# Output projections' last tiles on banks of their own, and the Vector work around them in a different order

## The reference, cut to what matters

```python
for i in range(DEPTH):
    h = _rmsnorm(x, attn_norm[i])
    x = x + mixer_i(h, ...)            # attention, then o @ w_o (1024 x 1024)
    x = x + swiglu_ffn(_rmsnorm(x, ffn_norm[i]), w_gate[i], w_up[i], w_down[i])
return _rmsnorm(x, final_norm)
```

## Time and profile before

| | us |
|---|---|
| median of 3 runs | 1173.62 (1172.78 to 1173.78) |
| the profiled execution | 1172.65 |
| its span, first to last instruction | 1170.8 |
| mean granted TensorE clock over the span | 0.998 |

### The profile page before, as it was taken

The page is one execution under the profiler, slowest core; times in us unless marked ns, Lnnn a source line. Parts: engine busy times, 40 slices in busy tenths (PEclk is TensorE's granted clock), DMA queues, the critical chain, the costliest instruction groups (busy, mean ns, idle before and its releaser), DMA issues.

```text
span 1170.8 us, 18043 instructions
## 1 busy us (share of the span) xinstructions
PE 1155.0 (99%) x7336; PEld 1030.4 (88%) x7336; DVE 800.4 (68%) x864; ACT 632.5 (54%) x753; POOL 276.4 (24%) x251
## 2 busy tenths in 40 slices
PE   9999999999999999999999999999999999999997
PEld 7989988888997888888899888888889999888886
DVE  5786777775589667776558777766556867776642
ACT  6775565554455556555336746555346755655532
POOL 2200532211123354221111354221110005322100
PEclk9999999999999999999999999999999999999999
DMA  8743555555552346556553245555545335555650
GB/s 330 191 143 109 180 179 195 182 202 191 179 171 104 111 177 216 181 181 216 180 180 136 98 166 214 183 179 213 183 172 186 108 109 181 180 188 181 223 182 36
DMA packets 31260, 202.36 MB, mean 173 GB/s; under 512 B 3552, under 2 KB 4640, under 8 KB 7760
## 3 DMA queue, kind: packets, MB, share of 16 engines
q1 hardware_dynamic: 28800, 196.88, 47.7%
q10 hardware_dynamic: 2032, 3.07, 0.9%
q0 software_dynamic: 352, 1.31, 0.8%
HBM read 198.43 MB, written 1.84 MB: 171 GB/s over the span
## 4 chain that ended last, share of the span: by engine, by line
PE 93%; DVE 3%; ACT 2%; DMA 1%; SPq 1%; issue 1%; POOL 0%; ACTq 0%; DVEq 0%
PE banks L1321 38%; PE banks L1325 20%; PE banks L1309 9%; PE banks L1315 7%; PE banks L1317 6%; PE banks L1316 6%; PE banks L1447 1%; PE banks L1389 1%; DMA raw<-w 1%; PE banks L1461 1%; ACT w_hi L487 0%; PE banks L1449 0%; PE banks L1601 0%; DVE small L1147 0%; SPq L313 0%
## 5 line engine op out<-in xcount | busy, mean ns | idle before, releaser
L851 DVE TENSOR_TENSOR w_lo<-raw,w_hi 128x2048 fp32r<-128x2048 f32 x180 | 442.1, 2459 | 206.2 <-ACT w_hi L487 206.1
L487 ACT ACTIVATE w_hi<-raw 128x2048 fp32r<-128x2048 f32 x183 | 349.2, 1909 | 94.7 <-PE banks L1317 35.7
L1321 PE MATMUL banks<-x_split,w_hi 128*128 128x512 f32 x1408 | 336.7, 391 | 0.0
L1321 PEld LDWEIGHTS banks<-x_split,w_hi 128*128 128x128 f32 x1408 | 258.6, 188 | 49.8
L1325 PEld LDWEIGHTS banks<-x_split,w_lo 128*128 128x128 f32 x1408 | 181.1, 191 | 7.1
L1325 PE MATMUL banks<-x_split,w_lo 128*128 128x256 f32 x1408 | 184.0, 284 | 0.0
L1321 PE MATMUL banks<-hid_split,w_hi 128*128 128x512 f32 x528 | 129.9, 392 | 0.0
L1321 PEld LDWEIGHTS banks<-hid_split,w_hi 128*128 128x128 f32 x528 | 95.6, 188 | 17.4
L1315 PE MATMUL banks<-x_split,w_hi 128*128 128x256 f32 x384 | 110.8, 288 | 0.0
L1316 PE MATMUL banks<-x_split,w_hi 128*128 128x256 f32 x384 | 108.7, 283 | 0.0
L1317 PE MATMUL banks<-x_split,w_lo 128*128 128x256 f32 x384 | 108.7, 283 | 0.0
(11 more groups left out here) (194 smaller groups left out, 1573.7 us busy)
## 6 DMA issues: line engine op xcount, KB each, us to landing
raw<-w SPq DMA_DIRECT2D x183, 1024.0 KB, 4.9
raw<-w SPq DMA_DIRECT2D x8, 256.0 KB, 6.7
x<-x_in SPq DMA_DIRECT2D x4, 256.0 KB, 6.5
raw<-w SPq DMA_DIRECT2D x2, 512.0 KB, 7.9
k_all<-k_all ACTq DMA_DIRECT2D x1, 960.0 KB, 8.3
rel_scratch<-rel_lut POOLq DMA_DIRECT2D x1, 768.0 KB, 10.0
rel_bias<-rel_scratch POOLq DMA_DIRECT2D x2, 256.0 KB, 9.8
y_gain<-final_rows ACTq DMA_DIRECT2D x1, 512.0 KB, 3.5
```

Source lines behind the costliest of these rows:

```text
L487: act.activation(w_hi[slot][:, :], raw[slot][:, :], ACT.Copy).then_inc(hi_done, 1)
L851: dve.tensor_tensor(w_lo[slot][:, :], raw[slot][:, :], w_hi[slot][:, :].bitcast(FP32), ALU.subtract).then_inc(lo_done, 1)
L1321: return pe.matmul(pair(b), wt[0], xs, start=first, stop=False, skip_group_check=True)
```

## The change

The bank table and the signal that counts finished even tiles:

```diff
-GATE_BANKS, UP_BANKS, DOWN_BANKS, OUT_LAST_BANK = (0, 2), (4, 6), (2, 3), 3
+GATE_BANKS, UP_BANKS, DOWN_BANKS, LAST_BANKS = (0, 2), (4, 6), (2, 3), (2, 3, 6, 7)
-        norm = signals("norm", "six x_new hi lo ss sums ms guess rstd")
+        norm = signals("norm", "even x_new hi lo ss sums ms guess rstd")
```

VectorE's `out_projection`: tiles 4 to 7 have two adds, with a wait between them (`step`), and the low part of the first up unit is written ahead of add 6:

```diff
                 def add(t):
-                    if t == 6:
-                        dve.wait_ge(norm.six, i + 1)
+                    if t in (4, 6):
+                        dve.wait_ge(norm.even, 2 * i + t // 2 - 1)
                     else:
                         dve.wait_ge(unit_used, u + t // 2 + 1)
-                    src = bank[OUT_LAST_BANK][:, 0:SEQ] if t == 7 else pair(4 + t // 2 % 2)[:, t % 2, :]
+                    if t >= 4:
+                        step(dve.tensor_tensor(x[:, t, :], pair(LAST_BANKS[t - 4])[:, 1, :], x[:, t, :], ALU.add))
+                    src = pair(LAST_BANKS[t - 4])[:, 0, :] if t >= 4 else pair(4 + t // 2)[:, t % 2, :]
...
                 norm_lo(n, 5)
+                split(u + SPLIT_SLOTS + 2)
                 add(6)
                 norm_lo(n, 6)
                 add(7)
                 norm_lo(n, 7)
-                split(u + SPLIT_SLOTS + 2)
                 split(u + SPLIT_SLOTS + 3)
```

TensorE: tiles 4 to 7 run as `high_halves` over all k and then `low_half` over all k, tile 4 in bank 2, 5 in bank 3, 6 in bank 6, 7 in bank 7, with no wait for a bank:

```diff
-            def out_rest(i):
-
-                done, u = 16 * i, FFN_BASE[i] - 2
-                pe.wait_ge(norm.x_new, done + 2)
-                two_tiles(u, 4, o_tile)
-                pe.wait_ge(lo_done, u + 2)
-                pe.wait_ge(norm.x_new, done + 4)
+            def rest_high(i, t, tiles):
+                slot, base = (FFN_BASE[i] - 4 + t // 2) % 3, t % 2 * KT
+                if t % 2 == 0 and tiles[0] == 0:
+                    pe.wait_ge(lo_done, FFN_BASE[i] - 3 + t // 2)
+                for k in tiles:
+                    high_halves(LAST_BANKS[t - 4], w_tile(slot, base + k), o_tile(k), k == 0)
+
+            def rest_low(i, t):
+                slot, base = (FFN_BASE[i] - 4 + t // 2) % 3, t % 2 * KT
                 for k in range(KT):
-                    last = product(bank[5][:, 0:SEQ], w_tile((u + 1) % 3, k), o_tile(k), k == 0, k == KT - 1)
-                last.then_inc(norm.six, 1)
-                for k in range(KT):
-                    last = product(bank[OUT_LAST_BANK][:, 0:SEQ], w_tile((u + 1) % 3, KT + k), o_tile(k), k == 0,
-                                   k == KT - 1)
-                last.then_inc(unit_used, 1)
+                    last = low_half(LAST_BANKS[t - 4], w_tile(slot, base + k), o_tile(k), k == KT - 1)
+                last.then_inc(unit_used if t % 2 else norm.even, 1)
+
+            def out_rest(i, begun=0):
+
+                for t in range(4, KT):
+                    rest_high(i, t, range(begun if t == 4 else 0, KT))
+                    rest_low(i, t)
```

TensorE at the end of a stick-breaking layer: one piece of cover goes from ahead of `keep_sums` to behind it, and five of tile 4's high matmuls go ahead of the two pieces that wait for the last part of o:

```diff
                         out_part(i, 0, range(4, 6))
-                        out_part(i, 1, range(0, 6))
+                        out_part(i, 1, range(0, 5))
                     keep_sums(p)
+                out_part(i, 1, range(5, 6))
                 out_part(i, 0, range(6, 7))
                 values(KT - 1)
                 out_part(i, 1, range(6, 7))
+                rest_high(i, 4, range(0, 5))
                 out_part(i, 0, range(7, 8))
                 out_part(i, 1, range(7, 8))
-                out_rest(i)
+                out_rest(i, 5)
```

## The result

| | kernel before | changed kernel |
|---|---|---|
| median of 4 runs, us | 1173.49 (1172.78 to 1173.78) | 1185.26 (1184.26 to 1186.32) |
| ratio, 95% interval | | 1.0105 (1.0093 to 1.0117) |
| span of the profiled execution, us | 1170.8 | 1182.9 |
| mean granted TensorE clock | 0.998 | 0.994 |

Slower, as forecast, but by 11.8 us (12.3 by the ratio) and not 5.8, and outside the range. The waits of TensorE come first, in the form of rows 9; the first row is new.

What follows compares the result with a forecast made beforehand. TensorE, busy 99%, was taken to bound the kernel, with VectorE's chain making it wait at the joins. Joins of 1.7, 1.2, 0.9 and 1.7 us plus 0.3 gave 5.8 us on 1172.65, plus 0.97 to the median: 1179.4 us, range 1176.4 to 1182.4.

Steps and rivals of the forecast that it cites:

- TensorE's side: Before the gate unit: shorter matmul stream starts it sooner by 1.35 us in layers 0 and 3, 0.75 and 0.45 in 1, 2.
- The waiting part: At each join TensorE waits for norm_lo: 1.7, 1.2, 0.9 and 1.7 us later, 5.5 in sum, 5.8 with 0.3 added.
- 0.3 in all on top: Added to the joins' sum because the up unit's low-part write can run longer beside GpSimd: 0.3 us.
- I count 0.45 of the 0.9 us: Second adds of tiles 4 and 5 on VectorE, partly hidden by norm_lo 4's 0.25 us wait; bounds 0.35 and 0.9.
- the low part in layer 2: Up unit's low part moved ahead of add 6 on VectorE: 2.29 us alone, 0.07 covered, so 2.2 us extra.
- the resuming: TensorE restarting after a wait: 0.15 us after the releasing end, plus 0.1 us for the slower first matmul.
- 0.35 and 0.2 us: End of stick-breaking: 0.35 us from earlier exp and `values`, up to 0.2 from o's covered last low part; counted as 0.6.
- the bounds that it lists: Per join -0.1 to +0.45 us and restart's 0.25 left out: 5.8 - 1.4 and 5.8 + 1.8, and GpSimd's 1.6 us.
- the dismissal of the clock: Rival, behind the joins: clock falls to 1.2 GHz for one 5.58 us unit per join, about 1202 us; chance 0.02.
- TensorE's saving: Rival, at the joins: VectorE stays ahead, joins come sooner by 3.9 us in all, 1169.7 us; chance 0.08.
- GpSimd stayed in VectorE's way: Its opposite was the rival: norm_lo's separated from GpSimd's squares, 1.3 to 1.6 us back per join, 1173.6 us; chance 0.06.
- its squares: Rival, after norm_lo 7: GpSimd's sums of squares become TensorE's next wait, 0.4 us per join more, 1181.0 us; chance 0.08.

Runs made afterwards that it cites:

- experiment 2: Changed kernel with unread matmuls in only one of TensorE's two gate-unit waits: 1179.36 us, 1.0059 (only before k = 7); 1179.44 us, 1.0062 (only before k = 6).
- Experiments 1 and 2: Changed kernel with unread matmuls in TensorE's gate-unit waits: in both waits 1179.50 us, ratio 1.0056; in one wait only 1179.36 us, 1.0059, and 1179.44 us, 1.0062.
- experiment 5: Kernel before with one edit, the first up unit's low part ahead of add 6: 1174.20 us, ratio 1.0013 to the kernel before.

## Why the prediction was wrong

**The direction and the mechanism held.** TensorE's side did start the gate unit sooner (1.29 us in layer 0 for the forecast 1.35), VectorE's chain decided, TensorE waited at k = 6 and k = 7 for L876, no GpSimd wait took its place, and nothing was given back. Second adds start 0.45 us after the first, as rows 6 had it, and an add that does not need the one in front 0.34 us after it (127.07 and 127.41 us). The Trainium skill (VectorE: DVE Perf Modes, section "The DRAIN you can't avoid") has a semaphore cost nothing extra; the trace disagrees for these adds, by 0.1 us.

**The waiting part was sized about 1 us too small.** With the clock kept up by fillers the change costs 0.56 to 0.62%, 6.6 to 7.3 us, for the forecast 5.8, which is still inside each of the three intervals. The traces agree with the larger number: join by join, the start of the up unit moves by 2.0, 1.5, 1.75 and 2.0 us from the kernel before to the one with fillers (layer 0 corrected by the 0.36 us by which the latter is ahead at 48 us), where 1.7, 1.2, 0.9 and 1.7 were forecast, and 0.3 in all on top. Two terms were small. One is "I count 0.45 of the 0.9 us" for the adds of tiles 4 and 5: norm_lo 5 now ends at 129.85, 1.41 us later than before, of which 0.6 is the later start, so the term is 0.8 us, near the bound of 0.9. The 0.25 us of waiting ahead of norm_lo 4 that was to hide them is gone from the row at 128.21, but norm_lo 4 and 5 themselves now take 1.64 us. The other is the low part in layer 2, 2.2 us by forecast, where the next add now comes 2.74 us after it starts:

```profile
681.93 2.82 DVE L851 TENSOR_TENSOR w_lo<-raw,w_hi 128x2048 fp32r<-128x2048 f32 x1
684.67 0.41 DVE L909 TENSOR_TENSOR x<-banks,x 128x256 f32<-128x256 f32 x1
```

Against them stands the resuming, forecast at 0.25 us with the slower first matmul: k = 7 starts 0.05 us after norm_lo 7's end (135.81 and 135.76), so with that matmul it is 0.15. Two slips in the working did not matter: 0.35 and 0.2 us are 0.55 and not 0.6, and the bounds that it lists give 1178.0 to 1181.2 us, or up to 1182.8 with GpSimd's 1.6, where the stated range is 3 us to each side. The result lies outside both.

**The step that failed is the dismissal of the clock.** The prediction had it as a rival at 0.02, because "in the only idle stretch of this size, 1.66 us, the granted clock of the window stayed 1.00". That row was read rightly, and experiment 2 confirms it for a single stretch. But it is evidence on one stretch, and the prediction itself forecast two of 1.5 us each with 0.46 us of matmuls between; it never asked what the pair does. Experiments 1 and 2 show that the pair lowers the clock where neither of its waits alone does, at a price of some 5 us; without it the result would have been about 1180 us, inside the range. A clock below 1.00 behind the joins was among the prediction's own signs of being wrong. The rival's price was off as well, 5.6 us per join in all four; measured are 1.5 to 1.6 us in three. The Trainium skill (TensorE: Matmul & The Clock Gate, Part 1) describes the clock as falling to half after idle time, and the trace agrees as to the two levels, 1.00 and 0.50; that two gaps with work between them can do it is shown by these runs alone.

**The other rivals.** TensorE's saving did not count (0.08), GpSimd stayed in VectorE's way (0.06), and its squares never held TensorE in the joins (0.08).

## What to carry to other kernels

A share of 68% says nothing of an engine's slack at a join: read, row against row, how far each of its results is ahead of the matmul that wants it, and spend that lead once only. Here 2.6 us were to be had and the change asked for 4. When TensorE will wait at several points close together, price the waits together and leave room for a fallen clock: a few unread matmuls in the holes took back some 5 of 12 us, and showed which part was waiting and which was clock. Of a change in several parts run the parts: here the new banks and the new order at the end of the mixer, with one add per tile, were worth 0.2%, hidden under 1.2% of loss.

## What the runs showed of the hardware that was not expected

- Two idle stretches of TensorE, with 0.7 us of matmuls between them, lowered the granted clock to 0.50 in three of four joins: 1.72 and 1.12 us in layers 0 and 3, 0.57 and 1.13 us in layer 1. A stretch of 1.71 or of 1.12 us alone never did in the joins of two kernels, four executions each.
- With 0.90 and 1.00 us the clock fell in layer 0 and not in layer 3 of one and the same execution, and the eight executions of that kernel differ in their mean clock (0.996 to 0.998) and, with it, in their time.
- The low part of a weight unit took 2.28 us in layer 0 of the changed kernel, where GpSimd had been idle since 129.57 us. It took 2.82 us where it started while GpSimd was still summing squares: in layer 2 of the changed kernel and in layer 0 of experiment 5. So its place in VectorE's order also sets its length.
